# Small experts of a two-layer encoder trunk: unsplit fp32 weights in two 64-column tiles, whole gates, then ups, then downs

## The reference, cut to what matters

```python
def moe_swiglu(x, w_router, w_gate, w_up, w_down):
    t = x.reshape(B * S, D)
    logits = (t @ w_router).astype(jnp.float32)
    top_vals, top_idx = lax.top_k(logits, TOP_K)
    top_w = jax.nn.softmax(top_vals, axis=-1)
    gates = jnp.sum(jax.nn.one_hot(top_idx, N_EXPERTS) * top_w[..., None], axis=1)
    out = jnp.zeros_like(t)
    for e in range(N_EXPERTS):   # w_gate[e], w_up[e]: 1024 x 1792, w_down[e]: 1792 x 1024, float32
        out = out + gates[:, e:e + 1] * ((silu(t @ w_gate[e]) * (t @ w_up[e])) @ w_down[e])
    return out
```

## Time and profile before

| what | value |
|---|---|
| median of 3 runs | 1126.77 us (1126.63 to 1127.04) |
| the profiled execution's own time | 1126.51 us |
| its span | 1124.7 us |
| PE busy | 1101.6 us (98%), 5470 instructions |
| DVE busy | 877.7 us (78%) |
| ACT busy | 749.8 us (67%) |
| PE's granted clock | 0.999 of full speed over the span |
| transfers | 294.94 MB, mean 262 GB/s; over 400 GB/s in most of the last third |

### The profile page before, as it was taken

One profiled execution on the slowest core, in us unless ns is written; L12 is line 12 of the kernel. 1 busy time (PEld: TensorE's weight loads), 2 busy tenths in 40 slices (PEclk: granted clock), 3 DMA queues, 4 the chain that ended last, 5 costly groups with the idle time before them and its releaser, 6 DMA issues.

```text
span 1124.7 us, 15463 instructions
## 1 busy us (share of the span) xinstructions
PE 1101.6 (98%) x5470; PEld 927.3 (82%) x5470; DVE 877.7 (78%) x1053; ACT 749.8 (67%) x921; POOL 39.5 (4%) x84
## 2 busy tenths in 40 slices
PE   9999999999999999999999999999899999999996
PEld 8888877888888888888877888887688887888875
DVE  6568877765445456568877689999998999999997
ACT  6545767454444446456766457899978898988785
POOL 3002000000000001002001000000000000000000
PEclk9999999999999999999999999999999999999999
DMA  9765534687555354655535649999999999999993
GB/s 327 270 159 181 183 106 130 188 274 253 197 183 182 127 181 148 198 144 185 170 121 168 205 149 333 372 418 413 418 418 354 380 402 410 404 417 405 412 365 140
DMA packets 135496, 294.94 MB, mean 262 GB/s; under 512 B 25486, under 2 KB 50156, under 8 KB 134908
## 3 DMA queue, kind: packets, MB, share of 16 engines
q1 hardware_dynamic: 134016, 288.23, 71.4%
q0 software_dynamic: 960, 5.28, 1.2%
q10 hardware_dynamic: 444, 0.47, 0.1%
HBM read 292.90 MB, written 1.05 MB: 261 GB/s over the span
## 4 chain that ended last, share of the span: by engine, by line
PE 77%; DVE 17%; DMA 2%; ACT 2%; issue 2%; ACTq 0%; SPq 0%; DVEq 0%
PE bank L1827 22%; PE bank L1829 21%; PE bank L1828 21%; DVE w_lo L1602 11%; DVE w_lo_more L1602 3%; PE bank L2259 2%; PE bank L2260 2%; PE bank L2079 2%; PE bank L1873 1%; DMA raw<-in_moe_w_gate 1%; PE bank L2059 1%; PE bank L2067 1%; DVE hid_buf L1741 1%; PE bank L2242 1%; ACT w_hi L1022 1%
## 5 line engine op out<-in xcount | busy, mean ns | idle before, releaser
L1243 DVE TENSOR_TENSOR w_lo<-raw,w_hi 128x1024 fp32r<-128x1024 f32 (+4 forms) x141 | 238.0, 1693 | 135.2 <-ACT w_hi L772 134.4
L772 ACT ACTIVATE w_hi<-raw 128x1024 fp32r<-128x1024 f32 (+5 forms) x141 | 201.5, 1432 | 144.1 <-PE bank L1829 144.1
L1602 DVE TENSOR_TENSOR w_lo<-raw,w_hi 128x1792 fp32r<-128x1792 f32 (+3 forms) x148 | 286.6, 1965 | 10.5 <-ACT w_hi L1022 9.6
L1022 ACT ACTIVATE w_hi<-raw 128x1792 fp32r<-128x1792 f32 (+3 forms) x148 | 244.0, 1666 | 44.6 <-PE bank L1829 31.2
L1827 PE MATMUL bank<-w_hi,aT_hi 128*128 128x512 f32 (+1 forms) x592 | 238.3, 403 | 0.8 <-DVE w_lo L1377 0.7
L1829 PE MATMUL bank<-w_hi,aT_lo 128*128 128x512 f32 (+1 forms) x592 | 229.8, 388 | 0.0
L1828 PE MATMUL bank<-w_lo,aT_hi 128*128 128x512 f32 (+1 forms) x592 | 229.5, 388 | 0.0
L1827 PEld LDWEIGHTS bank<-w_hi,aT_hi 128*128 128x128 f32 x592 | 111.3, 188 | 22.9 <-DVE w_lo L1377 1.0
L1829 PEld LDWEIGHTS bank<-w_hi,aT_lo 128*128 128x128 f32 x592 | 111.1, 188 | 22.7
L1828 PEld LDWEIGHTS bank<-w_lo,aT_hi 128*128 128x128 f32 x592 | 111.3, 188 | 21.0
L1602 DVE TENSOR_TENSOR w_lo_more<-raw,w_hi_more 128x1792 fp32r<-128x1792 f32 (+3 forms) x50 | 96.8, 1942 | 4.6 <-ACT w_hi_more L1022 4.6
(11 more groups left out here) (339 smaller groups left out, 1796.8 us busy)
## 6 DMA issues: line engine op xcount, KB each, us to landing
raw<-in_moe_w_gate SPq DMA_DIRECT2D x128, 448.0 KB, 6.6
raw<-in_moe_w_up SPq DMA_DIRECT2D x128, 448.0 KB, 6.5
raw<-in_moe_w_down SPq DMA_DIRECT2D x112, 512.0 KB, 6.7
raw<-in_w_in SPq DMA_DIRECT2D x40, 768.0 KB, 4.3
raw<-in_dense_w_gate SPq DMA_DIRECT2D x22, 512.0 KB, 3.8
raw<-in_dense_w_up SPq DMA_DIRECT2D x22, 512.0 KB, 4.6
raw<-in_dense_w_down SPq DMA_DIRECT2D x11, 1024.0 KB, 4.9
raw<-in_w_in SPq DMA_DIRECT2D x20, 512.0 KB, 4.6
```

Of the source, the lines that this page charges most:

```text
L772: act.activation(dst, src, ACT.Copy).then_inc(hi_made[j], 1)
L1022: act.activation(split_of(hi_slot, m), raw_of(i, n), ACT.Copy).then_inc(e_hi_made, 1)
L1243: dve.tensor_tensor(dst, src, high, ALU.subtract).then_inc(lo_made[j], 1)
L1602: dve.tensor_tensor(split_of(lo_slot, m), raw_of(i, n), split_of(hi_slot, m).bitcast(F32), ALU.subtract).then_inc(e_lo_made, 1)
```

## The change

Small experts: their weights are not split. A raw granule is multiplied as fp32 by 64 tokens' fp32 values, and two such matmuls go into the two 64-column halves of the array: for gate and up the two halves of the hidden columns (rows 0 to 63 and 64 to 127 of one bank), for down the two halves of the output columns. The fold is gone. The order of granules is new: a small expert's step 2e holds its 16 gate granules, step 2e+1 its 16 ups, and step 2e+2 (behind the next expert's first 16 granules) its 14 downs. A large expert keeps 8 gates and 8 ups per step and its 7 downs one step later, except that the first half of the seventh expert's downs stay one step later and the second half move behind the last expert's ups (step 15). A raw slot of a small expert's granule is free only when PE has used it. `pair_lo` moves from ACT to DVE, where it adds the low part of small experts' tokens to `x_small` in place. The silu and the product of gate and up run once for a small expert, on all 128 rows; its output is one bank, 128x512.

```diff
+def step_work(k):
+    gate_up, down = [], []
+    if k < STEPS and is_small(k):
+        gate_up = [(("gate", "up")[k % 2], k // 2, c, half) for c in range(KC) for half in range(2)]
+    elif k < STEPS:
+        gate_up = [(matrix, k // 2, c, k % 2) for matrix in ("gate", "up") for c in range(KC)]
+    for done in range(STEPS):
+        e, half = done // 2, done % 2
+        if not is_small(done):
+            at_step = STEPS - 1 if done == STEPS - 3 else done + 1
+            down += [("down", e, c, half) for c in range(HK)] if k == at_step else []
+        elif half and k == done + 1:
+            down += [("down", e, c, of) for of in range(2) for c in range(HK)]
+    return list(enumerate(gate_up)) + [(GU_N + n, what) for n, what in enumerate(down)]
...
+    both = [x for x in (i, i + 1) if not unsplit(x)]
...
+for m, (i, n) in enumerate(SPLITS):
+    last = i + n - 1
+    at = max(-1 if W_BEFORE[last] is None else W_BEFORE[last], last - W_SLOTS)
+    if at >= last // PER_ROUND * PER_ROUND:
+        SPLITS_BEHIND.setdefault(at // 2, []).append(m)
...
-            [("xT", [P, KC, 4 * P], F32R)])
+            [("xT", [P, KC, 2 * P], F32R), ("x_small", [P, KC, P])])
...
+                            elif unsplit(RAW_BEFORE[i]):
+                                sp.wait_ge(e_used, RAW_BEFORE[i] + 1)
                             else:
                                 sp.wait_ge(e_lo_made, SPLIT_OF[RAW_BEFORE[i]] + 1)
...
+            def pair_lo(r, p, q, b):
+                dve.wait_ge(x_lo_tr, 4 * (PAIRS_E * r + p) + q + 1)
+                dve.wait_ge(x_hi_in, 4 * (PAIRS_E * r + p) + q + 1)
+                for x in (1, 0):
+                    if is_small_expert(p, x):
+                        whole = x_small[:, 2 * q:2 * q + 2, small_at(p, x)]
+                        last = dve.tensor_tensor(whole, whole, tokens_of(p, x, b), ALU.add)
+                    else:
+                        last = dve.tensor_copy(xT[:, 2 * q:2 * q + 2, P:2 * P], tokens_of(p, x, b))
+                last.then_inc(x_lo_in, 1)
...
-            def add_folded(r, k, banks, part):
...
+                rows, cols_of = slice(0, P), slice(u * NB, (u + 1) * NB)
+                if is_small_expert(p, x):
+                    rows, cols_of = slice(u * SMALL, (u + 1) * SMALL), slice(0, NB)
...
+            def whole_gate_up(r, k, n):
+                i = SEQ[r, k, n]
+                matrix, e, c, _ = WORK[k, n]
+                wait_banks(r, k, matrix, c)
+                tokens = x_small[:, c, small_at(e // 2, e % 2)]
+                for half in range(2):
+                    pe.wait_ge(e_raw_in[(i + half) % RAW_SLOTS], 16 * ((i + half) // RAW_SLOTS + 1))
+                for u in range(2):
+                    for half in range(2):
+                        last = pe.matmul(bank[(B_GATE if matrix == "gate" else B_UP)[u]][half * SMALL:(half + 1) * SMALL, 0:HN], tokens,
+                                         raw_of(i + half)[:, 0, u * HN:(u + 1) * HN], start=c == 0, stop=c == KC - 1, skip_group_check=True)
+                last.then_inc(e_used, 2)
...
+            def whole_down(r, k, n):
...
+                pe.wait_ge(e_raw_in[i % RAW_SLOTS], 16 * (i // RAW_SLOTS + 1))
+                slots = hT_small[:, c * P + half * SMALL:c * P + (half + 1) * SMALL]
+                for u in range(2):
+                    last = pe.matmul(bank[B_Y[0]][u * SMALL:(u + 1) * SMALL, :], slots, raw_of(i)[:, 0, u * NB:(u + 1) * NB],
+                                     start=half == 0 and c == 0, stop=half == 1 and c == HK - 1, skip_group_check=True)
+                last.then_inc(e_used, 1)
```

More of the change, by code:

```diff
@@ L181 @@
+W_AT = {i: at for at, i in enumerate(W_ORDER)}
 H_SLOTS = (2, 3, 4, 5)
 def h_slots_read(r, slots):
[L186 to L197, removed]
-        BETWEEN[k + 1, n] = ("hidden", k, q)
+    return max(i for i in range(PER_ROUND * r, PER_ROUND * (r + 1)) if (i + RAW_SLOTS // 2) % RAW_SLOTS in slots) + 1
@@ L201 @@
+for k in range(STEPS - 1):
+    if not is_small(k):
+        hidden_between(k, 3, 9)
+    elif k % 2:
+        hidden_between(k, *((3, 9) if k % 4 == 1 else (5, 9)))
+for q, n in enumerate((GU_N + 2, GU_N + 4)):
+    BETWEEN[STEPS - 1, n] = ("hidden", STEPS - 1, q)
 for p in range(PAIRS_E):
@@ L1791, in between @@
                         b = B_X[TURN[what] % 2]
-                        if kind == "hidden" and m < STEPS - 1:
+                        if kind == "hidden" and not is_small(m):
                             hidden_lo_half(r, m, q, b)
+                        elif kind == "tokens_lo":
+                            pair_lo(r, m, q, b)
                         elif kind == "back":
@@ L2257, in small_product @@
-            def small_product(dst, x, b_hi, b_lo, start, stop):
-                pe.matmul(dst, x, b_hi, start=start, stop=False)
-                return pe.matmul(dst, x, b_lo, start=False, stop=stop)
-            def add_folded(r, k, banks, part):
-                s = small_steps(r, k)
-                for u in range(2):
-                    pe.wait_ge(e_fold_made, 4 * s + 2 * part + u + 1)
-                    last = pe.matmul(bank[banks[u]][:, 0:HN], shift[:, :], fold[:, u * HN:(u + 1) * HN], start=False, stop=True, skip_group_check=True)
-                last.then_inc(e_folded, 1)
@@ new lines, in hidden_half_transposes, with wait_banks @@
+                for n, c in enumerate(range(4) if q == 0 else range(4, HK)):
+                    last = pe.transpose(bank[b][:, n * P:(n + 1) * P], hid_buf[:, c * P:(c + 1) * P], ident[:, :])
+                last.then_inc(e_hid_tr, 1)
+            def wait_banks(r, k, matrix, c):
+                if k % 4 == 0 and c % 2 == 0 and matrix == "gate":
+                    pe.wait_ge(x_lo_in, 4 * (PAIRS_E * r + k // 4) + c // 2 + 1)
+                if k % 4 == 0 and c == 0 and matrix == "gate":
+                    pe.wait_ge(x_hi_in, 4 * (PAIRS_E * r + k // 4) + 4)
+                if c == 0 and (r or k):
+                    if matrix == "gate":
+                        pe.wait_ge(e_silu_made, silu_so_far(r, k))
+                    else:
+                        pe.wait_ge(e_hid_made, hidden_so_far(r, k))
```

379 lines of the change are left out of this document (160 added, 219 removed).

## The result

The changed kernel takes 1145.5 us in the median of 4 runs (1143.7 to 1148.3), against 1126.7 us before: a ratio of 1.017 (95% interval 1.0147 to 1.0193). It is slower by 19 us; 1113 us was forecast, with a range of 1104 to 1124 us. The profiled execution took 1143.66 us, its span is 1141.9 us.

A forecast was written before the change was run, and what follows sets the result against it. The expert stage was taken as transfer-bound, within 4% of 416 GB/s. Last landing 1097.3 us, plus 4 us to the last bring-back and 10.0 to the end, is 1111.3 us of span; with 1.8 around it 1113 us, range 1104 to 1124.

The forecast's parts named there:

- PE's cost per small expert: Small experts' fp32 pairs: 0.77 us for 448 columns, 0.88 for 512, 37 us per expert; PE's total unchanged within 2 us.
- the rival of tiles that don't overlap: Each pair in small experts: tiles taking turns need 1.54 us a pair, +130 us, 1243 us; chance 0.03.
- both forms: Small experts' pairs: tiles taking turns (1243 us, chance 0.03), or weight loads not hidden (1.33 us a pair, 1193 us, 0.02).
- Relief of DVE and ACT: Small experts' splits removed: over 195 us of ACT and 230 us of DVE, by itself nothing where transfers run at 416 GB/s.
- The start, 726 us: First small gate at 723 us: no load issued until 724.6 us, first bytes at about 726 us.
- The shorter lead: Small granules: loads run at most 12 ahead of PE instead of 12 + 8; 5 us of transfer time lost, at most 12.
- the lead of 12 starves the transfers: Rival, expert stage: mean rate stays 400 GB/s, last landing 1107 us, total 1123 to 1126 us; same within 2.3 us: 0.08.
- The tail: Behind the last landing: 4 us to the last bring-back instead of 11.3, then 10.0 us unchanged; gain 7 us.
- a cover for the last hidden values: Step 15: seven large downs, 9.2 us of PE, cover the last expert's wait of a few us for silu, product and transposes.
- The granted clock: Sign of a wrong prediction: PE's clock, 1.00 before the change, falls while PE waits for transfers.

The follow-up runs named there:

- e5: The changed kernel with 14 raw slots instead of 12 and 6 split slots instead of 8: 1131.6 us.
- e2: The changed kernel with 16 raw slots instead of 12 and 6 split slots instead of 8: 1122.65 us.
- e9: The changed kernel (12 raw slots) with the large experts' third product (x_lo by w_hi) cut to 64 columns, left out in the last chunk: 1124.0 us.
- e12: The kernel before the change with 16 raw and 6 split slots instead of 12 and 8: 1160.7 us.
- e15: The kernel before the change with 12 raw slots as before and 6 split slots instead of 8: 1161.4 us.
- e6: e2 with the second half of the seventh expert's downs put back from step 15 into step 14: 1121.7 us.
- e10: e2 with the first two large granules behind each run of small ones split one by one instead of as a pair: 1119.4 us.
- e7: e2 with both the edit of e6 (downs back in step 14) and that of e10 (single splits): 1115.7 us.
- e11: e7 with the seventh expert's four bring-backs moved ahead of the last expert's downs: 1114.3 us.
- e4: The changed kernel with the first two large granules behind each run of small ones split one by one instead of as a pair: 1141.2 us.
- e3: The changed kernel with added matmuls of zeros in seven chunks of the ups of steps 5, 11 and 15, to keep the clock up: 1144.1 us.

## Why the prediction was wrong, point by point

**PE's cost per small expert: right.** Pairs were to be 0.77 us for 448 columns and 0.88 for 512. In the dense stretches of the timeline, where four pairs of either kind are 16 instructions or five pairs 20:

```profile
772.22 3.16 PE bank L2310 x16
...
1114.63 4.51 PE L2339 MATMUL bank<-raw,fold 128*64 128x512 f32 x20 [2.28 <-DVE y_lo L1744]
```

3.16 / 4 = 0.79 us and 4.51 / 5 = 0.90 us: 38 us per small expert, where 37 were taken. (The first line is from the chain, the second from the timeline.) The tiles run side by side and their weight loads are hidden, so the rival of tiles that don't overlap is out in both forms, though the kernel did get slower, as that rival had it. "TensorE: Matmul & The Clock Gate" of the Trainium skill (part 3, "The mechanism") says that a load overlaps running matmuls only where its row group differs. That is not borne out here: at 0.79 us a pair has no room for four loads of 0.14 us laid bare. The same section also names a background weight buffer into which a load may be pulled ahead, and with that the rows agree.

**Relief of DVE and ACT: right, and worth nothing by itself,** as said: 238 and 222 us fewer.

**The start, 726 us: nearly right.** From 726 us at 416 GB/s, the window from 723 to 740 us would show 14/17 of it, 343 GB/s; it shows 296, some 2 us more lost.

**The shorter lead: this is the step that failed.** The term was "5 us of lost transfer time in all", at most 12. From 726 us at 416 GB/s the last landing would be at 1092 us; it was at 1120.5, so 28 us were lost. The rest of the miss is in the tail (below): 23.2 us of landing and 7.6 us of tail, less 0.2 behind it, are the 30.6 us between the 1111.3 us of span forecast and 1141.9. Two things in the step were wrong.
First, it measured PE's lag only at the ends of two large experts, and credited the 14 small downs in their midst with giving 5.3 us back. Those downs make the deepest hole of all, 242 GB/s: their transfers are ahead of PE by the whole of the large granules before them, and a lead of 12 ends while PE is still there. What cheap granules give back on PE is of no use when the queue has run dry before it.
Second, it took a lag of six granules as free (12 slots, six of latency) and counted only what is over. But the list changes its kind 15 times, not twice, and at each of the seven entries into large granules PE starts from nothing split, 4 to 6 us behind the landing. e5 and e2 put the price at some 6 and 4.5 us per slot: a lead that were enough nearly everywhere would show no such slope. By e9, PE's lag in large experts makes some 15 us of the loss.
The rival "the lead of 12 starves the transfers" named the mechanism, and the text said what would show it: a dip at 720 to 727 us and near large experts. Its size was bounded by what the kernel before loses there. That was the wrong bound: in the kernel before a raw slot never waits for PE itself, only for the split, so no row of it could price this. (In e12 and e15, with six split slots, four more raw ones are worth 0.7 us.) What was missing was a walk through one period of the list (16 large granules, 14 small, 23 large) with SP 12 granules ahead of PE.

**The tail: wrong by 7.6 us.** Four us were taken from the last landing to the last bring-back; they were 11.6 (1120.5 to 1132.1 us), no better than before. From the timeline of the end:

```profile
1104.58 1.15 DVE L1761 TENSOR_TENSOR hid_buf<-sg_buf,bank 128x448 f32<-128x448 f32 x2
...
1113.16 1.41 DVE L1744 SCALAR_TENSOR_TENSOR y_lo<-bank,slot_gate,y_hi 128x512 fp32r<-128x512 f32 x2 [7.44 <-ACT y_hi L1168]
...
1132.11 0.51 PE L2268 MATMUL bank<-y_hi,selT 64*128 64x512 f32 x2
```

The last expert's 14 downs can only start when the seventh expert's result has left the banks, at 1114.6 us, 2.3 us after PE was done with it. Then PE has 14 x 0.90 us and four bring-backs to do, which end at 1130.1, so it ends 9.6 us behind the last landing. The prediction let PE run "1 to 3 us late" and had left out that wait and the four bring-backs. The same wait reaches back into the landing: while PE stands still it frees no raw slot, and from 1114 to 1117 us the transfers run at 40 GB/s, so the two terms are not independent. The seven downs in step 15, called a cover for the last hidden values, are the work whose result PE waits for. What they cost with 12 raw slots was not run. With 16, moving them back (e6) gave 0.9 us, which can't be told from nothing, and 3.7 us beside single splits (e10 to e7); moving the four bring-backs (e11) gave 1.4 us, within the spread.

**The granted clock.** The prediction is wrong "if PE's granted clock falls while it waits for transfers". It did fall: half speed (1.2 GHz) for 6.8 us each behind 820, 990 and 1096 us. Windows of the changed kernel:

```profile
818.00:820.00 2.00, 0.00 (x0) 0.00 (x0) 1.27 (x1) 1.55 (x2) 0.00 (x0) 0.95 1.02 416
820.00:822.00 2.00, 1.09 (x3) 1.05 (x4) 1.88 (x2) 1.45 (x2) 0.00 (x0) 0.50 1.03 419
```

The first two falls came while PE stood idle at an entry, the third 0.9 us after it had started on the large granules, behind an idle stretch of 1.9 us; the first large granules were then done at half speed. Each fall takes at most 3.4 us of PE's work (half of 6.8), 10 us in all, some of it just ahead of a stop of the transfers. The falls are not the main cause of the loss: e4 has none from 747 to 1101 us and takes 1141.2 us, e9 has a lower mean clock and takes 1124.0 us. What they add was not isolated.

## What to carry to other kernels

Where two kinds of work share one prefetch ring, look at the changes between them to find the depth that the ring needs: count how often they alternate, and for each change add up the transfer's latency, the consumer's lag and the time that the first item takes through the stages. Here, what was lost at the changes was not made up in the stretches between them. If a change takes a stage out of a pipeline (here the split), the buffers of that stage should go to the stage that now holds the data longest: 12 + 8 slots took 1145.5 us and 16 + 6 took 1122.65 us in the same memory. And relief of an engine that is not the limit gives no time: here 238 us less on DVE and 222 us less on ACT came with 19 us more.

## What the runs showed of the hardware that had not been expected

- Two fp32 matmuls of 64 stationary columns, in the two halves of the array, run fully side by side at 448 and 512 columns too: 0.79 and 0.90 us for a pair.
- PE's granted clock fell to half in a kernel whose PE is busy for 96% of the span: three times for 6.8 us inside the expert stage, after stretches with many short waits for transfers (PE busy 13.3 of the 20 us from 800 us). How busy PE was in such a window doesn't tell the cases apart: in e7, with 15.2 of 20 us, the clock did not fall before the last 7 us of the span (mean 0.997); in e3, with 16.8, it fell at 821 us.
- In the changed kernel's small experts, from 803 to 817 us, PE waits 0.4 to 0.5 us for each pair of granules while the transfers stand at their rate. That rate, 416 to 418 GB/s, was exceeded by no version here from 740 to 840 us.
